# The cosine product of k's tiles on VectorE instead of GpSimd, in a two-layer gated trunk

## What is computed

```python
q = apply_rope(rms_norm(b_q.reshape(b, s, 4, 128), q_norm_g[l]), cos_q, sin_q)
k = apply_rope(rms_norm(b_k.reshape(b, s, 4, 128), k_norm_g[l]), cos_q, sin_q)
qi = apply_rope(i_q.reshape(b, s, 8, 64), cos_i, sin_i)
ki = apply_rope(i_k[:, :, None, :], cos_i, sin_i)[:, :, 0, :]

def apply_rope(x, cos, sin):
    x1, x2 = jnp.split(x, 2, axis=-1)
    return jnp.concatenate([x1 * c - x2 * s, x1 * s + x2 * c], axis=-1)
```

## Time and profile before

| what | value |
|---|---|
| runs | median 775.14 us (774.41 to 775.39, 3 runs) |
| the profiled execution | 773.44 us |
| its span, first to last instruction | 771.6 us |
| TensorE busy | 762.0 us (99%) |
| VectorE busy | 620.5 us (80%) |
| ScalarE busy | 460.7 us (60%) |
| POOL busy | 131.5 us (17%) |
| chain that ended last | TensorE 89%, VectorE 4%, ScalarE 4% |

### The profile page before, as it was taken

One profiled execution on the slowest core, in us unless ns is written; L12 is line 12 of the kernel. 1 busy time (PEld: TensorE's weight loads), 2 busy tenths in 40 slices (PEclk: granted clock), 3 DMA queues, 4 the chain that ended last, 5 costly groups with the idle time before them and its releaser, 6 DMA issues.

```text
span 771.6 us, 12228 instructions
## 1 busy us (share of the span) xinstructions
PE 762.0 (99%) x4364; PEld 666.3 (86%) x4364; DVE 620.5 (80%) x1051; ACT 460.7 (60%) x866; POOL 131.5 (17%) x125
## 2 busy tenths in 40 slices
PE   7999999999999999999999999999999999999998
PEld 7988878888899889988899788888889998999886
DVE  5767999999978884689986689999998878746895
ACT  5578786442577556735665977664335684676342
POOL 1344111000030103012215420300011101210130
PEclk9999999999999999999999999999999999999999
DMA  9838558522695529495874745893248844665784
GB/s 330 289 73 200 130 117 227 183 85 83 164 205 148 133 68 156 137 273 127 192 242 148 173 106 149 172 263 110 67 87 221 179 158 69 123 136 181 203 151 122
DMA packets 57900, 123.10 MB, mean 160 GB/s; under 512 B 3824, under 2 KB 8112, under 8 KB 57840
## 3 DMA queue, kind: packets, MB, share of 16 engines
q0 software_dynamic: 23568, 50.42, 34.6%
q1 hardware_dynamic: 33984, 71.31, 28.3%
q10 hardware_dynamic: 288, 0.59, 0.2%
HBM read 107.63 MB, written 10.49 MB: 153 GB/s over the span
## 4 chain that ended last, share of the span: by engine, by line
PE 89%; DVE 4%; ACT 4%; issue 2%; DMA 1%; ACTq 0%; DVEq 0%
PE bank L950 11%; PE bank L952 11%; PE bank L951 11%; PE bank L1020 7%; PE bank L1021 7%; PE bank L1019 7%; PE bank L1103 6%; PE bank L989 3%; PE bank L987 3%; PE bank L988 3%; PE bank L1048 3%; PE bank L1049 3%; PE bank L1050 3%; PE bank L924 2%; PE bank L942 2%
## 5 line engine op out<-in xcount | busy, mean ns | idle before, releaser
L1618 DVE TENSOR_TENSOR w_lo<-w_raw,w_hi 128x1024 fp32r<-128x1024 f32 x168 | 203.1, 1220 | 30.3 <-ACT w_hi L1190 25.4
L1190 ACT ACTIVATE w_hi<-w_raw 128x1024 fp32r<-128x1024 f32 x168 | 172.9, 1052 | 43.4 <-DMA w_raw<-in_w_out 18.9
L783 POOL DMA_DIRECT2D w_raw<-in_w_in x48 | 57.5, 1211 | 396.2 <-DVE w_lo L1618 371.5
L1019 PE MATMUL bank<-h_hi,w_lo 128*128 128x256 f32 x256 | 75.6, 295 | 0.0
L950 PE MATMUL bank<-h_lo,w_hi 128*128 128x512 f32 x192 | 75.5, 393 | 0.0
L952 PE MATMUL bank<-h_hi,w_hi 128*128 128x512 f32 x192 | 74.8, 389 | 0.0
L951 PE MATMUL bank<-h_hi,w_lo 128*128 128x512 f32 x192 | 74.7, 389 | 0.0
L1021 PE MATMUL bank<-h_hi,w_hi 128*128 128x256 f32 x256 | 72.4, 283 | 0.0
L1020 PE MATMUL bank<-h_lo,w_hi 128*128 128x256 f32 x256 | 72.4, 283 | 0.0
L1019 PE MATMUL bank<-hs,w_lo 128*128 128x256 f32 x192 | 56.3, 293 | 0.0
L1698 DVE MAX8 top<-score 128x8 f32<-128x256 f32 (+2 forms) x96 | 53.5, 558 | 3.4 <-DVE g_a L1863 1.8
(11 more groups left out here) (239 smaller groups left out, 1960.9 us busy)
## 6 DMA issues: line engine op xcount, KB each, us to landing
w_raw<-in_w_in SPq DMA_DIRECT2D x84, 512.0 KB, 4.5
w_raw<-in_w_in POOLq DMA_DIRECT2D x48, 512.0 KB, 6.7
w_raw<-in_w_out POOLq DMA_DIRECT2D x16, 512.0 KB, 6.7
w_raw<-in_w_out SPq DMA_DIRECT2D x12, 512.0 KB, 4.3
out<-x_sb POOLq DMA_DIRECT2D x4, 1024.0 KB, 5.8
w_raw<-in_w_oa SPq DMA_DIRECT2D x8, 512.0 KB, 3.7
w_raw<-in_w_ob SPq DMA_DIRECT2D x8, 512.0 KB, 4.1
x_sb<-out POOLq DMA_DIRECT2D x2, 2048.0 KB, 10.9
```

Of the source, the lines that this page charges most:

```text
L783: pool.dma_start(w_raw[:, slot], block_weights(layer, u), accum_op=ALU.add) \
L1019: nc.tensor.matmul(dst, w_lo[:, wk, col], a_hi[:, k], start=first and i == 0, stop=False, skip_group_check=True)
L1190: nc.scalar.activation(hi, w_raw[:, raw_slot(layer, u)], ACT.Copy).then_inc(s_whi.sem, 1)
L1618: nc.vector.tensor_tensor(lo, w_raw[:, raw_slot(layer, u)], hi.bitcast(F32), ALU.subtract) \
```

## The change

The cosine product of the four k tiles of each layer moves from POOL to VectorE, into the place where the q tiles' product already stands: right before the sine halves, on the same engine. `times_cos_gains` goes. The semaphore of the product is now counted for the four index tiles alone, and VectorE waits for it on those alone. POOL's waits for the staged tiles remain, with the transfers behind them.

```diff
-        s_cos = sig("tile_times_cos", 2 * TILES)
+        s_cos = sig("tile_times_cos", TILES)
...
-                def times_cos_gains(n, m):
-
-                    pool.wait_ge(s_rot.sem, s_rot.at(layer, n))
-                    nc.gpsimd.tensor_tensor(
-                        rope_a[:, 0:HEADS * DH].rearrange("p (h d) -> p h d", h=HEADS),
-                        stage[:, n % 2, 0:HEADS * DH].rearrange("p (h d) -> p h d", h=HEADS),
-                        rope_g[:, 1 - m // TILES, m % TILES, 0].unsqueeze(1).to_broadcast([P, HEADS, DH]),
-                        ALU.mult).then_inc(s_cos.sem, 1)
...
                     pool.wait_ge(s_stage.sem, s_stage.at(layer, TILES + n + 1))
-                    if n < TILES:
-                        times_cos_gains(TILES + n, n)
...
-                if n < 2 * TILES:
+                if n < TILES:
                     dve.wait_ge(s_cos.sem, s_cos.at(layer, n + 1))
...
-                    if m >= TILES:
-                        dve.wait_ge(s_rot.sem, s_rot.at(layer, n))
-                        vec.mark(nc.vector.tensor_tensor(
-                            rope_a[:, 0:HEADS * DH].rearrange("p (h d) -> p h d", h=HEADS),
-                            stage[:, n % 2, 0:HEADS * DH].rearrange("p (h d) -> p h d", h=HEADS),
-                            rope_g[:, 0, m % TILES, 0].unsqueeze(1).to_broadcast([P, HEADS, DH]), ALU.mult))
+                    dve.wait_ge(s_rot.sem, s_rot.at(layer, n))
+                    vec.mark(nc.vector.tensor_tensor(
+                        rope_a[:, 0:HEADS * DH].rearrange("p (h d) -> p h d", h=HEADS),
+                        stage[:, n % 2, 0:HEADS * DH].rearrange("p (h d) -> p h d", h=HEADS),
+                        rope_g[:, 1 - m // TILES, m % TILES, 0].unsqueeze(1).to_broadcast([P, HEADS, DH]), ALU.mult))
```

## The result

| | before | changed |
|---|---|---|
| median | 773.8 us (18 runs, 772.85 to 775.39) | 775.6 us (18 runs, 774.96 to 779.34) |
| ratio | | 1.003, 95% interval 1.0023 to 1.0038 |
| profiled span | 771.6 us | 775.1 us |
| stretch k to v, layer 0 and layer 1 | 69.57 and 69.47 us | 70.74 and 70.62 us |

The change makes the kernel slower by 0.3%, which is 2.3 us of 773.8 (1.8 to 2.9 us by the interval; the two medians differ by 1.8). The prediction was 2.3 us on a median of 775.14. The median of the kernel before came out lower over more runs, so the measured 775.6 lies just under the predicted range of 775.8 to 779.3, and the difference is what can be compared: the ratio applied to 775.14 gives 777.5, where 777.4 was forecast.

What follows compares the result with a forecast made beforehand. The prediction took TensorE, without slack against VectorE and ScalarE near the k tiles, as the bound. Per layer 0.41, 0, 0.61 and the rest of the last tile reach 1.17; 2 x 1.17 = 2.3 us gives 777.4, range 775.8 to 779.3.

Steps and rivals of the forecast that it cites:

- What bounds: Near the k tiles TensorE has no slack against the pair VectorE and ScalarE; from 79.16 the path hangs on VectorE.
- Removed and moved on POOL: Eight products of 1.28 us leave POOL, off the path; its later loads and terms start up to 1.28 us earlier: 0.
- Tile 0: k tile 0: product delays the reciprocal at 55.68 and ScalarE's stage; TensorE's matmul at 61.97 comes 0.41 us late.
- Tile 1: k tile 1: VectorE's idle 2.57 us behind it takes the product's 0.61 us back, so it adds 0.
- Tile 2: k tile 2: product delays the reciprocal at 68.92, which ScalarE waits for; adds 0.61, TensorE about 1.0 us late at 75.30.
- those waits are above 0, so slack is 0: Argument against gaps hiding the delay: TensorE's waits around 75.30, only a few tenths, leave it no slack.
- Tile 3: k tile 3: VectorE is 1.63 us late at 77.54, less 0.46 of slack before the q tile: 1.17 late at 79.16.
- The sum: Both layers alike, 2 x 1.17 = 2.3 us over the median of 775.14 us, giving 777.4 us.
- The rule against the trace: Trace: POOL's reads cost VectorE 0. Skill's blocking rule: 0.15 us overlaps given back, two a layer, sum 1.7 us.
- the gaps absorb it: Rival: slack hides the late reciprocal, only the first tile's 0.41 reaches TensorE; 0.8 us, 776.0 us; chance 0.20.
- every product lands in full: Rival: gaps before 65.74 and 79.16 don't absorb, 4 x 0.61 per layer; 4.9 us, 780.0 us; chance 0.14.
- the hand-over was the cost: Rival: the rotation really waited for POOL's product, so the change gains 8 x 0.59 = 4.7 us, 770.4 us; chance 0.04.

Runs made afterwards that it cites:

- both_engines: Changed kernel, with POOL also making the k products at its old place into an unread buffer, VectorE waiting for them: stretch 70.76 and 70.64 us, ratio 1.0042.
- k0_only: Kernel before, with only k tile 0's product moved to VectorE, the other three left on POOL: stretch 69.96 and 69.88 us.
- early_reciprocal: Changed kernel, with k tile 3's reciprocal moved on VectorE ahead of an index sum and a block sum: stretch 70.01 and 69.86 us, ratio 1.0015.
- k2_only: Kernel before, with only k tile 2's product moved to VectorE, the other three left on POOL: stretch 70.08 and 70.00 us.
- q_on_pool: Kernel before, with the q products moved to POOL too, so all eight k and q products are there: stretch 71.62 and 71.56 us, ratio 1.0049.
- k3_only: Kernel before, with only k tile 3's product moved to VectorE, the other three left on POOL: stretch 69.67 and 69.58 us.
- k1_only: Kernel before, with only k tile 1's product moved to VectorE, the other three left on POOL: stretch 69.65 and 69.48 us.
- earlier_sums: Kernel before, k products still on POOL, with VectorE's sums moved earlier into its idle times: stretch 69.10 and 68.87 us, median 772.23 us, ratio 0.9976.
- pool_reads_beside_q: Changed kernel, with POOL also making the q products into a buffer nobody reads: stretch 74.37 and 74.21 us, 784.00 us in a single run.

## Why the prediction was right

**What bounds.** Right: VectorE and ScalarE. The delay entered TensorE where it had a wait before, or came within tenths of one, but one of these places wasn't in the prediction (tile 0 below).

**Removed and moved on POOL: 0.** Right, both_engines shows it to 0.02 us of the stretch.

**Tile 0: 0.41.** Measured 0.39 and 0.41. The stage started at 56.69, less 0.20 for the start 56.49, as worked out. But the prediction had TensorE first late at 61.97, over the stage and the relu, and TensorE was late before that: its transposition at 57.95 waits for the index remainder `ki_lo`, which stands on VectorE behind the same product. That remainder came 0.44 us late (58.12 for 57.48, less 0.20) and the transposition with it, in the changed kernel and in k0_only (0.43). There were two ways for nearly the same delay, so that the number was right although one way was left out is in part luck. By this reading mending the reciprocal alone would not win tile 0 back; that wasn't tried.

**Tile 1: 0.** Measured 0.08 and 0.01.

**Tile 2: 0.61.** The way was right (early_reciprocal), the size a little high: 0.51 and 0.53. TensorE had about 0.1 us of slack at the load of 75.30, although it showed a wait of 0.22 us there, and "those waits are above 0, so slack is 0" was the step that didn't hold. The timeline of TensorE in the kernel before has the matmul of that load 0.22 us behind the one before it (75.34 and 75.12), the same as between its neighbours, so no time was lost by that wait; in k2_only the same two stand 0.46 us apart.

**Tile 3: 1.63 - 0.46.** Measured 0.10 and 0.11 alone, and 1.16 in all at 80.52.

**The sum.** 2 x 1.17 = 2.3 us; measured 2.32 in the stretches and 0.3% in the ratio. That the sum came out closer than its steps is in part luck: tiles 2 and 3, taken alone, were each a little smaller than forecast. That the single steps sum to 1.08 and the whole gives 1.17 fits the same slack: tile 2 pays it alone, and with tile 0 late it is paid already in part. This last reading is argued, not shown.

**The rule against the trace.** Here the working was weak. From one pair that overlapped by 0.15 us I took POOL's reads to cost VectorE nothing. For this change the sum stands, since POOL's k products lay where VectorE was idle or over its instructions by no more than 0.15 us, or beside ones that read one operand from PSUM. But as a statement on the chip it was wrong: beside a longer overlap VectorE's sum of two SBUF operands took 2.20 us for 1.22. The Trainium skill (SBUF — State Buffer, Who interferes with whom) says that such a pair contends and that the later one blocks fully. That they contend, the runs show. That the later one waits fits where POOL's product began first: overlaps of 0.15, 0.71 and 1.12 us lengthened VectorE's instruction by 0.01, 0.57 and 0.98. It doesn't fit q_on_pool, where a sum that had started 0.6 us before the product was the one that grew most (3.49 us); why, is open. An overlap that is too short to show anything is no evidence against a rule.

**The rivals.** That the gaps absorb it is refuted by k2_only and k3_only, that every product lands in full by k1_only, and that the hand-over was the cost by the sign.

## What to carry to other kernels

An instruction added to an in-order engine costs what the first waited-for instruction behind it can't absorb: between nothing and its whole length, tile by tile, and a small instruction that others wait for (a reciprocal of 0.17 us) belongs ahead of long ones that nobody waits for. Work that POOL does more slowly was free here while VectorE was idle, and dear where its reads lay beside VectorE's long sums of two SBUF operands, and beside one short instruction with a single one. Where an effect is a few tenths of a per cent, the length of a fixed stretch on the bounding engine within one profile tells more than whole times.

## What the runs showed of the hardware

- VectorE's tensor_tensor of two SBUF operands (128 x 1024) took 2.20 us in place of 1.22 where a tensor_tensor of POOL that reads SBUF had begun before it and lay over it by 1.1 us: the overlap is nearly all added. With an overlap of 0.71 us (earlier_sums) it took 1.79. Where the sum began first and the product 0.6 us later (q_on_pool, layer 1), the sum took 3.49 us, 2.27 more than alone, although the product took only 1.80. POOL's products took 1.33 to 1.80 us beside VectorE's work in place of 1.28, so POOL is slowed too.
- VectorE's tensor_scalar on 128 x 16, with one operand in SBUF, took 0.93 us in place of 0.17 beside a product of POOL, in both layers of q_on_pool and pool_reads_beside_q.
- Beside POOL's write of a constant, with some 0.4 us of overlap, two such sums took 2.59 us together, as without it.
- The same product costs VectorE 0.61 us start to start (0.69 us by its duration) and takes POOL 1.28 us.
